# First feed-forward weights in places of their own, and modulation rows turned by transposes

## What is computed

```python
def modulated_norm(x, g, shift, scale):
    return rmsnorm(x, g) * (1 + scale[:, None]) + shift[:, None]

def half_ffn(x, mod, g, w_up, w_down):
    h = modulated_norm(x, g, mod[:, 0], mod[:, 1])
    a, b = jnp.split(h @ w_up, 2, axis=-1)
    return x + FFN_RES * mod[:, 2][:, None] * ((jax.nn.silu(a) * b) @ w_down)
```

## Time and profile before

| | |
|---|---|
| median of 3 runs | 3224.68 us (3219.2 to 3228.15) |
| the profiled execution | 3225.6 us, its span 3223.9 us |
| PE, matmuls | busy 3152.0 us, 98% of the span |
| PE, weight loads | 2819.6 us (87%), beside the matmuls |
| DVE | 1155.8 us (36%) |
| ACT | 823.2 us (26%) |
| POOL | 138.6 us (4%) |
| moved by DMA | 390.85 MB, 121 GB/s on average |
| mean granted clock of PE | 0.988 of full speed |

### The profile page before, as it was taken

How to read it: one execution, slowest core, us unless ns; L and a number is a source line. 1 busy time by engine, 2 the same in 40 slices (tenths; PEclk the granted TensorE clock), 3 DMA queues, 4 the chain that set the end, 5 groups by cost and what they waited for, 6 DMA issues and landing times.

```text
span 3223.9 us, 54630 instructions
## 1 busy us (share of the span) xinstructions
PE 3152.0 (98%) x23756; PEld 2819.6 (87%) x23756; DVE 1155.8 (36%) x1943; ACT 823.2 (26%) x1211; POOL 138.6 (4%) x269
## 2 busy tenths in 40 slices
PE   8999999999999999999999999999999999999999
PEld 6999998877677899999999999988776778899999
DVE  3332334344432334333343323342544223443333
ACT  2221223333331222212222212242324212222121
POOL 0000000000412000000000000000003120000000
PEclk9999999999999999999999999999999999999999
DMA  6344432211258432332223444311122683222212
GB/s 243 131 168 173 153 122 83 90 53 46 88 173 269 128 119 85 135 147 108 90 79 131 164 177 148 128 56 69 50 75 63 206 282 99 110 79 86 98 70 77
DMA packets 118736, 390.85 MB, mean 121 GB/s; under 512 B 12785, under 2 KB 63313, under 8 KB 100321
## 3 DMA queue, kind: packets, MB, share of 16 engines
q1 hardware_dynamic: 100464, 338.36, 29.4%
q0 software_dynamic: 14432, 34.09, 3.1%
q10 hardware_dynamic: 3600, 14.91, 1.2%
HBM read 373.62 MB, written 13.69 MB: 120 GB/s over the span
## 4 chain that ended last, share of the span: by engine, by line
PE 90%; DVE 3%; ACT 3%; DMA 3%; issue 1%; SPq 0%; ACTq 0%; DVEq 0%
PE g L839 80%; PE q L839 5%; PE tb L839 4%; DMA w<-in_w_up 1%; DMA area<-in_w_ada 1%; ACT area L1782 1%; ACT area L1788 0%; DVE w_lo L1982 0%; DVE w_rest L1940 0%; ACT w_hi L1490 0%; PE tb L842 0%; DVE area L1909 0%; ACT w_hi_fill L1547 0%; DVE area L2172 0%; DMA area<-in_cache_v 0%
## 5 line engine op out<-in xcount | busy, mean ns | idle before, releaser
L839 PE MATMUL g<-h_hi,w_hi 128*128 128x272 f32 x2784 | 582.5, 290 | 16.9 <-ACT area L1499 9.7
L1490 ACT ACTIVATE w_hi<-w 128x1024 fp32r<-128x1024 f32 (+2 forms) x232 | 266.2, 1147 | 1259.0 <-PE g L839 950.6
L839 PE MATMUL g<-h_hi,w_lo 128*128 128x272 f32 x2784 | 577.4, 288 | 0.0
L839 PE MATMUL g<-h_lo,w_hi 128*128 128x272 f32 x2784 | 574.6, 287 | 0.0
L1982 DVE TENSOR_TENSOR w_lo<-w,w_hi 128x1024 fp32r<-128x1024 f32 (+2 forms) x232 | 309.9, 1336 | 511.9 <-ACT w_hi L1490 508.6
L839 PEld LDWEIGHTS g<-h_hi,w_hi 128*128 128x128 f32 x2784 | 438.1, 189 | 36.9 <-ACT area L1499 24.0
L839 PEld LDWEIGHTS g<-h_lo,w_hi 128*128 128x128 f32 x2784 | 437.6, 188 | 0.0
L839 PEld LDWEIGHTS g<-h_hi,w_lo 128*128 128x128 f32 x2784 | 436.8, 189 | 0.0
L839 PE MATMUL g<-h_hi,w_rest 128*128 128x272 f32 x1184 | 341.5, 291 | 0.0
L839 PE MATMUL g<-acts_hi,w_hi 128*128 128x272 f32 x1408 | 294.7, 290 | 0.0
L839 PE MATMUL g<-acts_hi,w_lo 128*128 128x272 f32 x1408 | 291.3, 288 | 0.0
(11 more groups left out here) (301 smaller groups left out, 4236.5 us busy)
## 6 DMA issues: line engine op xcount, KB each, us to landing
w<-in_w_up SPq DMA_DIRECT2D x44, 2048.0 KB, 7.8
w<-in_w_ada SPq DMA_DIRECT2D x32, 2048.0 KB, 7.7
w<-in_w_in SPq DMA_DIRECT2D x16, 2048.0 KB, 7.7
w<-in_w_down SPq DMA_DIRECT2D x16, 1536.0 KB, 6.6
w<-in_w_gate SPq DMA_DIRECT2D x48, 512.0 KB, 5.6
w<-in_w_down SPq DMA_DIRECT2D x16, 1280.0 KB, 5.5
area<-in_cache_k SPq DMA_DIRECT2D x72, 256.0 KB, 3.6
area<-in_cache_v SPq DMA_DIRECT2D x72, 256.0 KB, 4.3
```

The costliest lines, as they stand in the source:

```text
L839: return pe.matmul(o, a, b, start=start, stop=stop, skip_group_check=True, **kw)
L1490: ac.activation(WH[i % 2][:, 0:n], W[place][:, o:o + n], ACT.Copy).then_inc(s_wh, 1)
```

## The change

Two parts.

1. The high parts of blocks 0 and 1 get places of their own in the activations' buffer in every feed-forward (`MIDDLE_HI`, or `EARLY_HI` as before), and the low parts stand in the slot. The ring is thus free for blocks 2 and 3, whose splits now stand behind the norm on both engines, ahead of chunk 0. Behind them ACT runs a SiLU on one column. `release` waits for units 0 and 1 of the first step in all four feed-forwards.
2. `features` runs four transposes of 128x128 into a whole bank of `TB` in place of four matmuls with `fold`; DVE sums the four groups of each with a reduction from the bank, and then adds the bias.

```diff
--- before.py
+++ after.py
@@ -434,6 +434,7 @@
         assert o_f + 6 * T + 8 * P + KD * C <= AREA
         o_yb = 4 * T
         EARLY_HI = [over(f"w_hi_first{i}", (i * FF_PART[0] + FF_PART[1]) * T, 1024) for i in range(2)]
+        MIDDLE_HI = [over(f"w_hi_middle{i}", 4096 + i * 1024, 1024) for i in range(2)]
         FIRST_HI = [over(f"w_hi_a{i}", o, 1024) for i, o in enumerate((o_yb, o_yb + 1024, o_k, o_k + 1024))]
         UA_HI = EARLY_HI + FIRST_HI[2:4]
         LATER_HI = FIRST_HI[0:2] + [over(f"w_hi_b{i}", o_s + 1024 * i, 1024) for i in range(2)]
@@ -487,9 +488,8 @@
 
         def first_weights(l, f, i):
 
-            if l and not f:
-                return EARLY_HI[i][:, :], WR[AT["ffn", (l, f, 0)] % 2][:, i * UP_BLOCK:(i + 1) * UP_BLOCK]
-            return WH[i][:, 0:UP_BLOCK], WL[i][:, 0:UP_BLOCK]
+            hi = (EARLY_HI if l and not f else MIDDLE_HI)[i]
+            return hi[:, :], WR[AT["ffn", (l, f, 0)] % 2][:, i * UP_BLOCK:(i + 1) * UP_BLOCK]
 
         def const(name, rows=P):
             a, w = CONST_AT[name]
@@ -712,7 +712,7 @@
                     splits.n += FFN_UNITS[what[2]]
                     units.n += FFN_UNITS[what[2]]
                     sp.wait_ge(s_wl, splits.value())
-                    if what[0] and what[1:] == (0, 0):
+                    if what[2] == 0:
                         sp.wait_ge(s_unit, units.value() - 2)
                 elif what[1] in MIXER_UNITS:
                     units.n += MIXER_UNITS[what[1]]
@@ -880,7 +880,7 @@
                 if n >= 2:
                     pe.wait_ge(s_ada, n - 1)
                 for b in range(4):
-                    last = mm(TB[:, n % 2, b * C:(b + 1) * C], MR[:, n % 2, b * P:(b + 1) * P], fold, True, True)
+                    last = turn(TB[:, n % 2, b * P:(b + 1) * P], MR[:, n % 2, b * P:(b + 1) * P], ident)
                 last.then_inc(s_feat, 1)
 
             def product(p, blocks, rhs, m=P, first=None):
@@ -1446,6 +1446,10 @@
 
                 ac.activation(EPSC[:, 3:4], EPSC[:, 0:1], ACT.Sqrt, bias=ZERO[:, 0:1])
 
+            def silu_table():
+
+                ac.activation(EPSC[:, 3:4], EPSC[:, 0:1], ACT.Silu, bias=ZERO[:, 0:1])
+
             def first_hi(l, f):
 
                 at = AT["ffn", (l, f, 0)]
@@ -1493,12 +1497,14 @@
                     if ada[i] is not None:
                         rows(ADA_ORDER.index(ada[i]))
 
-                def chunk(c):
+                def chunk(c, ahead):
                     p = mine()
-                    split()
+                    if not ahead:
+                        split()
                     drained(ac.activation(halves(SIL[:, c % 2, :]), both(p), ACT.Silu, bias=ZERO[:, 0:1]), p)
                     mine()
-                    split()
+                    if not ahead:
+                        split()
 
                 if l or f:
                     roots(3 * l + 2 * f)
@@ -1506,11 +1512,14 @@
                     first_hi(l, f)
                 for k in range(KD):
                     hi_of_h(2 * f, k)
+                split()
+                split()
+                silu_table()
                 i = 0
                 for half, blocks in enumerate(FF_PART):
                     norm_next = half == 1 and (l + 1 < L or f == 0)
                     for c in range(blocks):
-                        chunk(c)
+                        chunk(c, half == c == 0)
                         if c % 2 == 1:
                             after(i)
                             i += 1
@@ -1950,7 +1959,9 @@
                 at4 = slice(4 * i, 4 * i + 4)
                 part, kind = divmod(i // 2, 3)
                 ve.wait_ge(s_feat, n + 1)
-                ve.tensor_tensor(MOD[:, at4, :], TB[:, n % 2, 0:4 * C].rearrange("p (b c) -> p b c", b=4),
+                link(ve.tensor_reduce(MOD[:, at4, :], TB[:, n % 2, :].rearrange("p (b g c) -> p b c g", b=4, g=4)[:, :, 0:C],
+                                      AX.X, ALU.add))
+                ve.tensor_tensor(MOD[:, at4, :], MOD[:, at4, :],
                                  BADA[:, l, at4][:, :, None].to_broadcast([P, 4, C]), ALU.add).then_inc(s_ada, 1)
                 ve.wait_ge(s_ada, n + 1)
                 half = slice(i % 2 * 4, i % 2 * 4 + 4)
@@ -1990,9 +2001,10 @@
                     while turned:
                         biased(turned.pop())
 
-                def chunk(c, m):
+                def chunk(c, m, ahead):
                     q = un.take()
-                    split()
+                    if not ahead:
+                        split()
                     p = mine()
                     ve.wait_ge(s_dr[q], un.d[q].value())
                     drained(ve.tensor_tensor(halves(PR), halves(SIL[:, c % 2, :]), both(p), ALU.mult), p)
@@ -2000,15 +2012,18 @@
                     link(ve.tensor_copy(AH[:, m, :], PR))
                     ve.tensor_tensor(AL[:, m, :], PR, AH[:, m, :], ALU.subtract).then_inc(s_acts, 1)
                     wait(acts)
-                    split()
+                    if not ahead:
+                        split()
 
                 if l == f == 0:
                     first_lo(l, f)
                 norm(3 * l + part)
+                split()
+                split()
                 i = 0
                 for half, blocks in enumerate(FF_PART):
                     for c in range(blocks):
-                        chunk(c, c)
+                        chunk(c, c, half == c == 0)
                         turn_over()
                         if c % 2 == 1:
                             after(i)
```

## The result

The changed kernel takes **3199.65 us**, the median of 4 runs (3199.35 to 3202.09), beside 3223.13 us before in the same rounds (4 runs, 3219.2 to 3228.15). The ratio is 0.9926, 95% interval 0.9908 to 0.9943: between 18 and 30 us less. Its profiled execution has a span of 3197.8 us, 26.1 less than the one before.

The account below looks back on a forecast made before the run. PE, on 90% of the chain, was taken to bound the kernel. Savings of 9.5 + 4.6 + 12.5 + 0.4 = 27.0 us from 3225.6 gave 3198.6, forecast as a median of 3198 us, range 3190 to 3211.

Parts of the forecast that it names:

- The holes: PE's four waits for the SiLU before unit 2 in the feed-forwards: each 2.37 us shorter, 9.5 us saved.
- rival (c): At the four SiLUs, a wait as long as the table load follows it: 5.2 us lost, 3203 us; chance 0.03.
- SP's next load: Weight load two steps on, behind SP's slot release: goes out earlier, not later; nothing counted.
- The clock at the holes: Low-clock stretches of unit 2 behind three of the four holes go: 1.54 us each, 4.6 us saved.
- The turned rows: Four transposes replace eight matmul passes per group of modulation rows: 0.39 us at 32 groups, 12.5 us saved.
- Rival (b): At the modulation rows, four transposes cost PE as much as the eight passes: 3211 us; chance 0.07.
- The reduction: DVE's sum behind each group's transposes: 0.30 us each, hidden in DVE's idle time at 32 groups.
- The race for the weights: PE's seven waits for low parts of weights stay at 5.6 us; shorter folds move both runners alike.
- The start: Four groups in a row at the kernel's start: last two gain, last pays the reduction; 0.4 us net saved.
- Rival (a): Low-clock stretches move elsewhere instead of going, so the 4.6 us is not won: 3203 us; chance 0.12.
- (d): PE's clock falls behind each of 32 transpose groups, up to 1.54 us each: 3247 us, slower; chance 0.03.
- (e): DVE or ACT reaches the early splits late, the stall stays, only 12.9 us is won: 3212 us; chance 0.03.

Follow-up runs that it names:

- e1: The changed kernel with the old fold (four matmuls of 9 columns and the add): 3210.62 us, ratio 0.9951 to the kernel before.
- e3: The changed kernel without the early SiLU table load (the one-column SiLU): 3189.26 us, one run.
- e5: The kernel before with 19 unread matmuls filling the hole behind units 0 and 1 of each feed-forward: 3219.06 us, ratio 0.9987 to the kernel before.
- e8: The changed kernel with DVE's reduction of each group done three times: 3198.34 us, one run.
- e4: The changed kernel with each group's four transposes run twice: 3206.51 us, one run.

## Why the prediction was right

The forecast was 3198 us and 27.0 us less in the profiled execution; measured were 3199.65 and 26.1. Point by point:

- **The holes, 9.5 us.** Right. 2.6 us became 0.2 at all four places, and e1 gives 9.5. That ACT and DVE just fit behind the norm held as well, with 0.2 us to spare. One sub-step was beside the point: I counted the early table load as needed, and e3 shows that the order of the splits does it alone. No 1.38 us of drain shows, not in the earlier trace rows and not here: ACT's small activation starts 1.30 us after the load, so rival (c) is out. The Trainium skill, "ScalarE: Activation LUTs", "What ACT_TABLE_LOAD costs", gives the 1283 ns that the trace shows, and the drain that it adds is not seen. The 6.31 us that I called the time of 48 matmuls is that from unit 2's start to ACT's next split; the 48 starts take 6.11. Nothing in the sum hangs on it.
- **SP's next load.** Earlier, as said. It was issued at 1670.41, 6.4 us behind the end of unit 0; now it goes out at 1647.96, 0.8 us behind it.

```profile
1670.41 0.33 SPq L757 DMA_DIRECT2D w<-in_w_up  x1
```

- **The clock at the holes, 4.6 us.** Right for this pair of profiles (three drops gone, 1.54 each); that the hole brings them is shown by e5, with no drop behind 4 filled holes. But the three were a draw: the kernel before has three or four, so the gain is 4.6 to 6.2.
- **The turned rows, 12.5 us.** The mechanism was right, the term of the sum mis-sized: 14.6 us, 0.46 a group instead of 0.39, and outside the 12 to 13 that I gave as its bounds. I counted a full step of 0.10 to 0.11 us for each of the four, 0.40 to 0.44 us. But the row of four lasts 0.60 us, with 0.27 for one of them: its last starts 0.33 us behind its first, and the next unit starts at 0.35. So only three steps count, and some 0.03 us for the last; the earlier trace rows already had this, seven steps of 0.11 and 0.03 in the 0.79 for eight. Rival (b) is out.
- **The reduction.** 0.301 us against the 0.30 that I worked out, and free, as e8 shows with three of them.
- **The race for the weights, "stay at 5.6".** Right in its mechanism: no transfer took the gain back, and shortening the fold moved both runners alike. "Late" is 6.1 and 5.7 us in the first two profiles. At the worst place before, a transfer of up weights of 9.15 us (issue to landing) made the unit 1.27 us late; at the worst one after, 9.17 us made it 1.28. Between two up steps of these profiles PE is over 0.5 us late only where the transfer took 8.5 us or more; the other transfers there took 7.5 to 8.2. Over all profiles "late" is 5.7 to 7.3 us with the old fold and 3.4 to 5.7 with the turned rows in the same order; whether the change has a part in that isn't settled. One reading was too kind: the 0.17 us "to spare" at 133.68 is nearly all the way from DVE to PE, since where PE waits it too starts 0.15 us behind the low part.
- **The start, 0.4 us.** Not resolved: the stage takes 48.2 to 52.6 us over all profiles, by when the first transfers land. The wait for the last add rose from 0.36 to 0.70 us, as counted.
- **Rival (a), the clock moves elsewhere.** In part what happened: between the two first profiles the mixers took back 4.0 us, 1.7 of it by the clock (54.6 and 58.0 us at the lower level, half of the difference); the rest wasn't traced. Two executions of the kernel before lie 13.1 us apart there, so 4.0 is within the draw and shows no effect of the change.

- **Rivals (d) and (e).** (d), the slower side, is out by e4: the clock is 1.00 behind each group of eight transposes, as behind each of four. The Trainium skill, "TensorE: Matmul & The Clock Gate", "Part 4: PE-mode transpose", has transposes not counting as busy; in short groups between dense matmuls these runs show no price of it. (e) is out by the timeline: the low parts of blocks 2 and 3 are ready at 1646.80, before unit 2 starts at 1647.93.

The sum again, as measured between the first two profiles: 9.5 for the holes, 4.6 for the clock, 14.6 for the rows, 0.4 for "late" and 0.6 at the start, less 4.0 in the mixers, is 25.7, against 26.1. That the forecast came so near is in part luck: the rows gained 2.1 us more than it had, and the mixers, which it left out, took 4.0 back.

## What to carry to other kernels

Where PE waits for an engine's first result, look at what stands in that engine's program between its last idle moment and this result. Work whose inputs have long been there can go ahead of the wait if it gets places of its own, and here the table load went with it. Price such a hole with the clock that PE may lose behind it; and read a gain of less than 1% from stages of the trace that the change touches, since untouched stages here vary by 13 us.

## What was not expected of the hardware

- A table load isn't held by the wait of the activation for which it is made: in e3 it is over 0.50 us before the wait ends.
- Four transposes between dense matmuls take 0.35 us, eight 0.80: the matmul behind them starts some 0.03 us after the last one does, not a step of 0.11.
- Behind the same hole of 2.6 us the clock fell 12 times in 16, with 1.54 us lost each time; how long the mixers run at the lower level (64.9 and 41.0 us) makes up some 12 of the 15 us between two executions of one program.
